# The first attention of a two-block transformer kernel, worked in pairs of heads

## The chip, the core and the metric

The kernel runs on one NeuronCore of one Trainium2 chip. The metric is the device time of one execution in microseconds (us). The engines are named as in the profile: PE is the TensorE matmul, PEld its weight load, DVE is VectorE, ACT is ScalarE, POOL is GpSimd and SP is SyncE, which here only issues DMAs. PEclk is the TensorE clock that the throttle granted, 1.00 for 2.4 GHz and 0.50 for 1.2 GHz.

## The reference

Two blocks of a transformer run over 256 tokens of width 1024. The change touches one place, the attention of the first layer (16 query heads of 64 channels, four key and value heads, each shared by four query heads). Cut to what matters, and without the batch axis:

```
q, k, v = split(x @ w_in); rotary embedding on q and k
score = sum over index heads of iw * relu(iq . ik / 8), causal
sel   = top 64 keys of each query by score           # a mask, the same for all 16 heads
for each of 16 heads h, with key head g = h // 4:
    logits = q_h k_g^T / 8, masked by sel and by causality
    p      = softmax(logits)
    o_h    = p v_g
out = concat(o_h) @ w_o
```

After it come layer norms, an MLP, a gated linear attention, a second MLP, and a second block with four branches (two of them attentions), cross attention and a feed-forward. None of these changes.

## The kernel before

Activations lie transposed: channels on the 128 partitions, 256 tokens along the free axis, in blocks of 128 channels (qT has 8 such blocks, so block p holds heads 2p and 2p+1, one in partitions 0 to 63, the other in 64 to 127). Weights stream through a ring of four SBUF buffers in 183 units of 16 tiles; ACT rounds each unit to whi (L906), DVE takes the rest wlo (L1307), and each product is three matmuls (L422 to L424). A product unit writes one of four PSUM banks, lin0 to lin3. JOB numbers every use of these banks in program order; the function bank makes PE wait until the fourth job before has been read out (semaphores evac0 to evac3), and filled makes a reader wait for job_done. Four more banks, att0 to att3, serve the attentions.

Each engine runs its own instruction stream, in the order in which it is written. The part in question:

1. The units of q (ups("q")), whose banks ACT copies to qT (L921), while DVE picks the 64 keys of each query (L1528, L1529) and makes the additive mask selbias.
2. Four rope steps for q, two blocks of qT each. PE multiplies by a permutation (L620), and DVE combines in three operations (L1495, L1496, L1498).
3. The 16 heads, one unit u each, over steps s = 0 to 18 (att_step). PE does the scores of unit s into att0 or att1, the transposes of unit s-2 into att2 and the values of unit s-3 into att3. In the scores only the 64 partitions of that head take part; the first half of the queries sees 128 keys, the second 256. kswap is kT with its two halves of partitions exchanged, for the heads whose keys lie in the other half. DVE (att_neg, L1436) adds the mask to the negated scores and takes their minimum; ACT (att_exp, L973) takes the exponential and, in a further instruction, its row sum; DVE (att_scale, L1445 to L1453) inverts the sums and scales the probabilities; ACT copies the transposes to SBUF (L982) and the result, after the values (L589), to qT (L987). Three of the four rope steps of DVE stand between its first heads.
4. keep_warm(9), nine matmuls on the identity that nobody reads (L497), and the units of the output projection ao. ACT splits qT to xh (L926) and DVE to xl (L1317), a quarter at a time, and the first unit (unit_first) waits for each quarter.

The matmuls on full fp32 operands (scores, values, keep_warm, rope) appear in the trace as two MATMUL records each, transposes as one.

Of the kernel before, what the change touches and what calls it, by code (L numbers as in the profile page):

```python
# [17 lines left out]
P = 128  # L18
S = 256
D = 1024  # L20
# [46 lines left out]
def plan():  # L67
# [24 lines left out]
    for i in range(4):  # L92
        add("rope", 4 + i)
# [88 lines left out]
def build(nc, units_d, x_d, mem_d, pos_d, vec_d, const_d, narrow_a_d, narrow_b_d, narrow_f_d, w_a2_d, b_fgt_d, lam_d, out_d):  # L182
# [4 lines left out]
    with ctx:  # L187
# [39 lines left out]
        def stage(*tensors):  # L227
# [4 lines left out]
         top8) = stage(  # L232
# [3 lines left out]
            ("selbias", [P, 2, S]), ("rbuf0", [P, 512]), ("rbuf1", [P, 512]), ("rtmp", [P, 2, S]), ("top8", [P, 8]))  # L236
# [46 lines left out]
        pT_psum, pT_sb, pv_psum, o_done = sem("pT_psum"), sem("pT_sb"), sem("pv_psum"), sem("o_done")  # L283
        z_summed, centered, squared, normed = sem("z_summed"), sem("centered"), sem("squared"), sem("normed")
# [71 lines left out]
        UNITS_ATT = [("A", i, None) for i in range(16)] + [("D", j, t) for j in range(4) for t in range(2)] \  # L356
            + [("F", i, None) for i in range(8)] + [("X", j, None) for j in range(4)]
        ATT0 = {k: [u[0] for u in UNITS_ATT].index(k) for k in "ADFX"}
# [10 lines left out]
        def att_rows(u):  # L369

            k, i, t = UNITS_ATT[u]
            return slice(64 * (i % 2), 64 * (i % 2) + 64) if k in "AF" else slice(0, P)
# [5 lines left out]
        def att_out(u):  # L378
            k, i, t = UNITS_ATT[u]
            return {"A": qT, "D": aqT, "F": fqT, "X": xqT}[k][att_rows(u), i // 2 if k in "AF" else i, att_cols(u)]  # L380
# [30 lines left out]
        def _(pe):  # L411
# [132 lines left out]
            def att_logits(u):  # L544
                k, i, t = UNITS_ATT[u]
                if free_after(u, "AFX"):
                    pe.wait_ge(neg_ready, free_after(u, "AFX"))
                for m in range(2):
                    o = att_scores(u, m)
                    w = att_keys(u, m)  # L550
                    q = slice((m if t is None else t) * P, (m if t is None else t) * P + P)
                    r = att_rows(u)
                    if k == "A":
                        pe.wait_ge(roped, 5 + i // 4)
                        keys = kT if i // 4 % 2 == i % 2 else kswap
                        last = mm(o, qT[r, i // 2, q], keys[r, i // 8, 0:w], start=True, stop=True)  # L556
                    elif k == "D":
# [18 lines left out]
            def att_values(u):  # L576
                k, i, t = UNITS_ATT[u]
                pe.wait_ge(pT_sb, u + 1)
                if free_after(u, "AF"):
                    pe.wait_ge(o_done, free_after(u, "AF"))  # L580
                for n, (m, b) in enumerate(att_blocks(u)):
                    o = att[3][att_rows(u), m * P:(m + 1) * P]
                    if k == "A":
                        v = v_tok[:, b, 64 * (i // 4):64 * (i // 4) + 64]
                    elif k == "F":
# [13 lines left out]


# [37 lines left out]
            for i in range(4):  # L638
                rope(4 + i, [JOB["q", i]], qT[:, 2 * i:2 * i + 2, :])
            pe.wait_ge(kswapped, 2)  # L640
            evacuated(pe, JOB["v", 0])
            for s in range(16 + 3):
                att_step(s, ATT0["A"], 16)
# [247 lines left out]
        def _(act):  # L891
# [134 lines left out]
            for s in range(16 + 3):  # L1026
                att_step(s, ATT0["A"], 16)
            split("ao", qT, lambda c: act.wait_ge(o_done, 4 * c + 4))
# [148 lines left out]
            act.wait_ge(o_done, 24)  # L1177
# [20 lines left out]
            for i in range(4):  # L1198
# [3 lines left out]
                if i == 0:  # L1202
                    branch_split(2, fqT, lambda c: act.wait_ge(o_done, 32))
# [80 lines left out]
        def _(dve):  # L1284
# [137 lines left out]
            def att_neg(u):  # L1422
# [5 lines left out]
                for m in range(2):  # L1428
                    w = att_keys(u, m)
                    if k == "A":  # L1430
                        mask = selbias[:, m, 0:w]
                    elif k == "X":
# [101 lines left out]
            for s in range(16 + 1):  # L1534
                att_step(s, ATT0["A"], 16)
                if s < 3:
                    rope(5 + s, two(qT, 1 + s))
                if s == 3:
                    next_low("q", 3)
            for c in range(4):  # L1540
# [499 lines left out]
```

## Time and profile before

| | us |
|---|---|
| median of 3 runs | 1396.02 |
| lowest, highest | 1394.32, 1397.08 |
| the profiled execution | 1394.16 |
| its span in the trace | 1392.3 |

| engine | busy, share of the span |
|---|---|
| PE | 95% |
| PEld | 91% |
| DVE | 67% |
| ACT | 45% |

In the 40 slices of the page PE is nearly full everywhere, and its clock is 0.9 or 1.0 in all but two slices: the third and fourth (about 70 to 140 us) show 7 and 5. The first attention lies there, from 83.2 to 144.5 us.

### The profile page before, as it was taken

The page shows a single profiled execution, that of the slowest core. Times are in us where ns is not written, and L with a number is a line of the kernel's source. Part 1 is how long each engine was busy: PE and PEld are TensorE (multiplying, and loading weights), DVE is VectorE, ACT ScalarE, POOL GpSimd, SP SyncE. Part 2 cuts the span into 40 slices and gives each one's busy share as a digit, 9 for nine tenths or more (in the row PEclk, how much of TensorE's full clock was granted, in tenths as well). Part 3 has the DMA queues.
Part 4 walks back from the last instruction along what each step waited for, and adds up shares of the span by engine and source line. Part 5 has one row for each costly group of instructions (what it writes and reads, how often), then busy time and mean ns, then how long its engine had stood idle before and what let it go on. Part 6 is the DMA issues. An engine that isn't in the chain of part 4 may idle for free.

```text
span 1392.3 us, 25125 instructions
## 1 busy us (share of the span) xinstructions
PE 1326.4 (95%) x10604; PEld 1272.3 (91%) x10604; DVE 928.1 (67%) x1448; ACT 627.4 (45%) x805; POOL 0.2 (0%) x4
## 2 busy tenths in 40 slices
PE   6889999999998899999999999999899999999897
PEld 6866999999998799999999999889898989999797
DVE  6783576466647767646665458888876665999943
ACT  5334454354444244534435444454445455555431
POOL 0000000000000000000000000000000000000000
PEclk9975999999999899999999999999999999999999
DMA  8320325545334133554532543334445241444430
GB/s 330 115 91 0 122 104 198 184 178 191 115 122 152 61 121 105 198 184 179 195 138 94 209 159 120 118 127 150 141 172 203 92 152 61 152 181 157 175 121 31
DMA packets 28361, 198.41 MB, mean 142 GB/s; under 512 B 3296, under 2 KB 3808, under 8 KB 4592
## 3 DMA queue, kind: packets, MB, share of 16 engines
q1 hardware_dynamic: 27072, 194.00, 38.7%
q10 hardware_dynamic: 1200, 3.14, 0.6%
q8 instruction: 66, 1.08, 0.3%
q14 instruction: 23, 0.19, 0.0%
HBM read 196.08 MB, written 1.05 MB: 142 GB/s over the span
## 4 chain that ended last, share of the span: by engine, by line
PE 69%; DVE 23%; ACT 3%; issue 3%; DMA 1%; DVEq 0%; ACTq 0%
PE lin L422 19%; PE lin L424 18%; PE lin L423 18%; DVE wlo L1307 7%; DVE conv L1748 3%; PE lin L504 2%; PE att L589 2%; PE att L497 2%; DVE fconv L1922 1%; PE att L556 1%; ACT whi L906 1%; PE att L573 1%; DVE fconv L1921 1%; DVE fconv L1923 1%; PE lin L527 1%
## 5 line engine op out<-in xcount | busy, mean ns | idle before, releaser
L422 PE MATMUL lin<-xh,whi 128*128 128x256 f32 x1936 | 556.2, 287 | 17.2 <-DVE xl L1317 11.8
L1307 DVE TENSOR_TENSOR wlo<-raw,whi 128x2048 fp32r<-128x2048 f32 x183 | 418.7, 2291 | 215.2 <-ACT whi L906 214.0
L423 PE MATMUL lin<-xl,whi 128*128 128x256 f32 x1936 | 550.8, 284 | 0.0
L424 PE MATMUL lin<-xh,wlo 128*128 128x256 f32 x1936 | 550.5, 284 | 0.0
L906 ACT ACTIVATE whi<-raw 128x2048 fp32r<-128x2048 f32 x183 | 348.5, 1906 | 179.5 <-PE lin L424 172.7
L422 PEld LDWEIGHTS lin<-xh,whi 128*128 128x128 f32 x1936 | 375.0, 194 | 21.4 <-DVE wlo L1307 10.6
L423 PEld LDWEIGHTS lin<-xl,whi 128*128 128x128 f32 x1936 | 375.0, 194 | 0.1
L424 PEld LDWEIGHTS lin<-xh,wlo 128*128 128x128 f32 x1936 | 374.5, 193 | 0.0
L422 PE MATMUL lin<-fh,whi 128*128 128x256 f32 x512 | 143.4, 280 | 0.0
L423 PE MATMUL lin<-fl,whi 128*128 128x256 f32 x512 | 142.8, 279 | 0.0
L424 PE MATMUL lin<-fh,wlo 128*128 128x256 f32 x512 | 142.8, 279 | 0.0
L424 PEld LDWEIGHTS lin<-fh,wlo 128*128 128x128 f32 x512 | 96.3, 188 | 0.0
L422 PEld LDWEIGHTS lin<-fh,whi 128*128 128x128 f32 x512 | 96.1, 188 | 0.0
L423 PEld LDWEIGHTS lin<-fl,whi 128*128 128x128 f32 x512 | 95.8, 187 | 0.0
L1748 DVE SCALAR_TENSOR_TENSOR conv<-upad,vec,conv 128x256 f32<-128x256 f32 x120 | 58.1, 484 | 3.9
L497 PE MATMUL att<-consts 128*128 128x128 f32 x464 | 57.0, 275 | 0.0
L422 PE MATMUL lin<-gh,whi 128*128 128x256 f32 x176 | 50.7, 288 | 6.4 <-DVE gl L1937 6.4
L497 PEld LDWEIGHTS att<-consts 128*128 128x128 f32 x464 | 54.6, 192 | 0.4 <-issue 0.2
L973 ACT ACTIVATE pr<-lg,nmax 128x128 f32<-128x128 f32 (+1 forms) x72 | 32.4, 452 | 48.5 <-DVE nmax L1436 43.5
L422 PE MATMUL lin<-whi,xh 128*128 128x256 f32 x176 | 50.7, 288 | 0.0
L423 PE MATMUL lin<-wlo,xh 128*128 128x256 f32 x176 | 50.5, 287 | 0.0
L424 PE MATMUL lin<-whi,xl 128*128 128x256 f32 x176 | 50.5, 287 | 0.0
(309 smaller groups left out, 1645.5 us busy)
## 6 DMA issues: line engine op xcount, KB each, us to landing
raw<-units_dram SPq DMA_DIRECT2D x183, 1024.0 KB, 4.8
h<-x_dram SPq DMA_DIRECT2D x1, 1024.0 KB, 6.8
memT<-mem_dram ACTq DMA_DIRECT2D x1, 1024.0 KB, 4.8
out_dram<-h SPq DMA_DIRECT2D x4, 256.0 KB, 2.0
consts<-consts_dram ACTq DMA_DIRECT2D x1, 867.5 KB, 12.2
narrow_a<-narrow_a_dram ACTq DMA_DIRECT2D x1, 544.0 KB, 14.1
vec<-vectors_dram ACTq DMA_DIRECT2D x1, 245.5 KB, 16.9
posi<-pos_dram ACTq DMA_DIRECT2D x1, 128.0 KB, 8.0
```

The source lines that it names most:

```text
L422: mm(out, w[0], a[0], start=first, stop=False)
L423: mm(out, w[0], a[1], start=False, stop=False)
L424: return mm(out, w[1], a[0], start=False, stop=last)
L497: mm(att[0][:, 0:P], ident, ident, start=True, stop=True)
L504: ins = mm(flat[:, (col + t) * width:(col + t + 1) * width], block[:, t * P:(t + 1) * P], ones[:, 0:width], start=first and t == 0, stop=l ...
L527: last = mm(o[:, n, t * P:(t + 1) * P], inv[:, col:col + 1].broadcast_to([P, P]), ident, start=True, stop=True)
L556: last = mm(o, qT[r, i // 2, q], keys[r, i // 8, 0:w], start=True, stop=True)
L589: last = mm(o, v, pT[u % 2][:, n, :], start=b == 0, stop=b == att_keys(u, m) // P - 1)
L906: f(whi[u % RING][:], raw[u % RING][:], ACT.Copy).then_inc(hi_ready, 1)
L973: last = f(pr[u % 2][:, m, 0:w], lg[u % 2][:, m, 0:w], ACT.Exp, scale=-1.0, bias=nmax[:, u % 2, m:m + 1], accum_out=rsum[:, u % 2, m:m + 1])
L1307: v.tensor_tensor(wlo[u % RING][:], raw[u % RING][:], whi[u % RING][:].bitcast(f32), ALU.subtract).then_inc(lo_ready, 1)
L1748: ins = v.scalar_tensor_tensor(out=conv[:, b, :], in0=x, scalar=w, in1=conv[:, b, :], op0=ALU.mult, op1=ALU.add)
```

## The change

The first attention leaves att_step and gets functions of its own that treat two heads, a pair p, in one step. The second block keeps the old code; there only the numbering of its units shifts.

- Scores of a pair (pair_scores) go to two banks of the lin ring, one for each head, and thus become two jobs. The four matmuls alternate between the heads, that is, between partitions 0 to 63 and 64 to 127.
- DVE (pair_neg) does what att_neg did, reads lin, and writes lg0, lg1 for an even pair and pr0, pr1 for an odd one.
- ACT (pair_exp) takes the exponential in place, without row sums. DVE no longer scales the probabilities.
- Transposes go to att0 for the even head and att1 for the odd one, after keep_warm(3) in each pair; ACT copies each to one of four buffers pT0 to pT3.
- The values (pair_values) go to att2 or att3. Beside v times the probabilities they form ones times the probabilities, the row sums, spread over 64 partitions. Each step is eight matmuls instead of the three of each head, of 256 or 128 columns, alternating between output partitions 0 to 63 and 64 to 127.
- DVE (pair_result) takes the reciprocal of the sums out of PSUM (128x256) and multiplies the result by it into qT; ACT's copy of the result goes.
- Two of the four rope products of PE move into steps 2 and 4. Where they stood there is keep_warm(14).

```diff
-    for i in range(4):
-        add("rope", 4 + i)
+    add("rope", 4); add("rope", 5)
+    for p in range(8):
+        if p in (2, 4):
+            add("rope", 5 + p // 2)
+        add("scores", p, banks=2)
...
+            ("pT2", [P, 4, P]), ("pT3", [P, 4, P]), ("amax", [P, 4, 2]), ("asum", [P, S]))
+        scores, apT = lg + pr, pT + [pT2, pT3]
...
+            def pair_scores(p):
+                pe.wait_ge(roped, 5 + p // 2)
+                j = JOB["scores", p]
+                o = [bank(j + e) for e in range(2)]
+                for m in range(2):
+                    w, q = P * (m + 1), slice(m * P, m * P + P)
+                    for e in range(2):
+                        r = slice(64 * e, 64 * e + 64)
+                        keys = kT if p // 2 % 2 == e else kswap
+                        last = mm(o[e][:, m, 0:w], qT[r, p, q], keys[r, p // 4, 0:w], start=True, stop=True)
+                        if m:
+                            last.then_inc(job_done, 1)
+            def pair_transposes(p):
+                for e in range(2):
+                    if p:
+                        pe.wait_ge(a_pT_sb, 2 * (p - 1) + e + 1)
+                    if e == 0:
+                        keep_warm(3)
+                    pe.wait_ge(a_exp, 2 * p + e + 1)
+                    for n, (m, b) in enumerate(((0, 0), (1, 0), (1, 1))):
+                        last = nc.tensor.transpose(att[e][:, n * P:(n + 1) * P], scores[2 * (p % 2) + e][:, m, b * P:(b + 1) * P], ident)
+                    last.then_inc(a_pT_psum, 1)
+            def pair_values(p):
+                pe.wait_ge(a_pT_sb, 2 * p + 2)
+                if p >= 2:
+                    pe.wait_ge(a_done, p - 1)
+                o = att[2 + p % 2]
+                for b in range(2):
+                    q0, n = b * P, 2 - b
+                    for at, w in ((0, v_tok[:, b, 64 * (p // 2):64 * (p // 2) + 64]), (S, ones[:, 0:64])):
+                        for e in range(2):
+                            t = apT[2 * (p % 2) + e][:, 2 * b:2 * b + n, :]
+                            last = mm(o[64 * e:64 * e + 64, at + q0:at + S], w, t, start=b == at == 0, stop=b == 1 and at == S)
+                last.then_inc(a_pv_psum, 1)
...
             ups("q")
-            for i in range(4):
+            for i in range(2):
                 rope(4 + i, [JOB["q", i]], qT[:, 2 * i:2 * i + 2, :])
             pe.wait_ge(kswapped, 2)
             evacuated(pe, JOB["v", 0])
-            for s in range(16 + 3):
-                att_step(s, ATT0["A"], 16)
+            keep_warm(14)
+            for s in range(8 + 2):
+                if s in (2, 4):
+                    i = 1 + s // 2
+                    rope(4 + i, [JOB["q", i]], qT[:, 2 * i:2 * i + 2, :])
+                if s < 8:
+                    pair_scores(s)
+                if 2 <= s:
+                    pair_values(s - 2)
+                if 1 <= s < 9:
+                    pair_transposes(s - 1)
+            pe.wait_ge(a_pT_sb, 16)
             keep_warm(9)
...
-            for s in range(16 + 3):
-                att_step(s, ATT0["A"], 16)
-            split("ao", qT, lambda c: act.wait_ge(o_done, 4 * c + 4))
+            def pair_exp(p):
+                j = JOB["scores", p]
+                for e in range(2):
+                    evacuated(act, j + e)
+                    sc = scores[2 * (p % 2) + e]
+                    for m in range(2):
+                        w = P * (m + 1)
+                        last = f(sc[:, m, 0:w], sc[:, m, 0:w], ACT.Exp, scale=-1.0, bias=amax[:, 2 * (p % 2) + e, m:m + 1])
+                    last.then_inc(a_exp, 1)
+            def pair_transposed(p):
+                for e in range(2):
+                    act.wait_ge(a_pT_psum, 2 * p + e + 1)
+                    if p >= 2 and e == 0:
+                        act.wait_ge(a_pv_psum, p - 1)
+                    f(apT[2 * (p % 2) + e][:, 0:3, :], att[e][:, 0:3 * P].rearrange("p (n q) -> p n q", q=P), ACT.Copy).then_inc(a_pT_sb, 1)
+            for s in range(8 + 1):
+                if s < 8:
+                    pair_exp(s)
+                if s:
+                    pair_transposed(s - 1)
+            split("ao", qT, lambda c: act.wait_ge(a_done, 2 * c + 2))
...
             rope(4, two(qT, 0))
-            for s in range(16 + 1):
-                att_step(s, ATT0["A"], 16)
-                if s < 3:
-                    rope(5 + s, two(qT, 1 + s))
+            def pair_neg(p):
+                j = JOB["scores", p]
+                for e in range(2):
+                    filled(dve, j + e)
+                    if p >= 2:
+                        dve.wait_ge(a_pT_psum, 2 * (p - 2) + e + 1)
+                    for m in range(2):
+                        w = P * (m + 1)
+                        last = v.tensor_tensor_reduce(out=scores[2 * (p % 2) + e][:, m, 0:w], in0=lin[(j + e) % RING][:, m, 0:w], in1=selbias[:, m, 0:w],
+                                                      scale=-64 ** -0.5, scalar=3.0e38, op0=ALU.add, op1=ALU.min, accum_out=amax[:, 2 * (p % 2) + e, m:m + 1])
+                    read_out(last, j + e)
+            def pair_result(p):
+                dve.wait_ge(a_pv_psum, p + 1)
+                if p:
+                    dve.wait_ge(a_done, p)
+                o = att[2 + p % 2]
+                link(v.reciprocal(asum[:], o[:, S:2 * S]))
+                v.tensor_tensor(qT[:, p, :], o[:, 0:S], asum[:], ALU.mult).then_inc(a_done, 1)
+            for s in range(8 + 2):
+                if s < 8:
+                    pair_neg(s)
+                if s in (0, 2, 4):
+                    rope(5 + s // 2, two(qT, 1 + s // 2))
                 if s == 3:
                     next_low("q", 3)
+                if s >= 2:
+                    pair_result(s - 2)
             for c in range(4):
                 low("ao", qT, c)
             residual("ao", "ln0")
```

In the order of instructions, without the counts of semaphores, one round of PE before is three matmul groups for one head. Here are two rounds (heads 3 and 4 scored, att the attention banks, pT the transposed probabilities):

```order
L556 MATMUL att1<-kswap,qT 128x128 [waits roped,neg_ready]
L556 MATMUL att1<-kswap,qT 128x256 [waits roped]
L573 MATMUL att2<-consts,pr1 128x128 [waits pT_sb,p_ready]
L573 MATMUL att2<-consts,pr1 128x128 x2
L589 MATMUL att3<-pT0,v_tok 64x128 [waits pT_sb]
L589 MATMUL att3<-pT0,v_tok 64x128 x2
L556 MATMUL att0<-kswap,qT 128x128 [waits roped,neg_ready]
L556 MATMUL att0<-kswap,qT 128x256 [waits roped]
```

In the changed kernel, the round in which pair 2 is scored and pair 0 gets its values, on PE as well:

```order
L612 MATMUL lin3<-kswap,qT 128x128 [waits evac0,evac3,roped]
L612 MATMUL lin0<-kT,qT 128x128
L612 MATMUL lin3<-kswap,qT 128x256
L612 MATMUL lin0<-kT,qT 128x256
L639 MATMUL att2<-pT0,v_tok 64x256 [waits a_pT_sb]
L639 MATMUL att2<-pT1,v_tok 64x256
L639 MATMUL att2<-pT0,consts 64x256
L639 MATMUL att2<-pT1,consts 64x256
L639 MATMUL att2<-pT0,v_tok 64x128
L639 MATMUL att2<-pT1,v_tok 64x128
L639 MATMUL att2<-pT0,consts 64x128
L639 MATMUL att2<-pT1,consts 64x128
```

The two heads' matmuls now stand next to each other, and the scores wait for ring banks (evac) instead of neg_ready. On DVE, the start of the attention before: rope for block pair 1 stands behind the mask operation of head 0.

```order
L1436 ISA lg0,nmax<-att0,selbias 128x128 [waits lg_ready,roped]
L1436 ISA nmax 128x1
L1436 ISA lg0,nmax<-att0,selbias 128x256
L1436 ISA nmax 128x1
L1495 TENSOR_TENSOR rtmp<-lin1,sinT 128x512 [waits job_done]
```

And DVE in the changed kernel around steps 2 and 3, with the second rope of the stage, the first result and the mask operations of pair 3:

```order
L1564 TENSOR_TENSOR rtmp<-lin2,sinT 128x512 [waits job_done]
L1565 TENSOR_TENSOR qT<-qT,cosT 128x512
L1567 TENSOR_TENSOR qT<-qT,rtmp 128x512 [waits evac2,dve_step]
L1621 RECIPROCAL asum<-att2 128x256 [waits a_pv_psum,roped]
L1622 TENSOR_TENSOR qT<-att2,asum 128x256 [waits dve_step]
L1611 ISA pr0,amax<-lin1,selbias 128x128 [waits a_pT_psum,job_done]
```

The result of pair s-2 stands behind the rope and in front of the mask operations of pair s+1.

## Rows read from the trace of the kernel before

**Rows 1.** The page: span, engines, and the chain that ended last.

```profile
span 1392.3 us, 25125 instructions
PE 69%; DVE 23%; ACT 3%; issue 3%; DMA 1%; DVEq 0%; ACTq 0%
```

**Rows 2.** Windows of the attention: length, busy PE, PEld, DVE, ACT, POOL; PEclk; DMA; GB/s.

```profile
85.00:87.00 2.00, 0.83 (x4) 0.43 (x4) 1.93 (x4) 0.88 (x4) 0.00 (x0) 1.00 0.10 41
87.00:89.00 2.00, 0.82 (x3) 0.50 (x3) 1.96 (x9) 0.98 (x4) 0.00 (x0) 0.65 0.00 0
95.00:120.00 25.00, 25.00 (x85) 16.46 (x85) 10.63 (x50) 11.27 (x40) 0.00 (x0) 0.50 0.12 42
142.00:143.00 1.00, 1.00 (x8) 0.66 (x7) 0.00 (x0) 0.38 (x1) 0.00 (x0) 0.90 0.00 0
```

**Rows 3.** Timeline of PE, the attention: start, duration (us), instruction, idle time before.

```profile
78.36 3.60 PE L620 MATMUL lin<-qT,consts 128*128 128x512 f32 x8
...
83.17 0.34 PE L556 MATMUL att<-kT,qT 64*128 64x128 f32 x1 [1.21 <-DVE qT L1498]
...
83.73 0.38 PE L556 MATMUL att<-kswap,qT 64*128 64x256 f32 x1
84.92 0.92 PE L556 MATMUL att<-kT,qT 64*128 64x128 f32 x4 [0.81 <-DVE nmax L1436]
...
93.75 1.65 PE L556 MATMUL att<-kswap,qT 64*128 64x128 f32 x4
95.33 0.90 PE L573 MATMUL att<-consts,pr 128*128 128x128 f32 x3
96.16 1.54 PE L589 MATMUL att<-pT,v_tok 128*64 128x128 f32 x6
97.63 1.65 PE L556 MATMUL att<-kT,qT 64*128 64x128 f32 x4
...
142.44 0.55 PE L573 MATMUL att<-consts,pr 128*128 128x128 f32 x3
142.92 1.52 PE L589 MATMUL att<-pT,v_tok 128*64 128x128 f32 x12
144.37 2.27 PE L497 MATMUL att<-consts 128*128 128x128 f32 x18
146.40 0.36 PE L422 MATMUL lin<-xh,whi 128*128 128x256 f32 x1
```

**Rows 4.** Timeline of PE, two levels of the gated linear attention, output halves alternating.

```profile
430.50 1.15 PE L694 MATMUL lin<-qk 128*64 128x64 f32 x32 [1.68 <-DVE qk L1615]
...
462.24 1.92 PE L694 MATMUL lin<-gqT,gkT 128*64 128x64 f32 x32
```

**Rows 5.** Timeline of DVE: rope, mask operations, the rest of a weight unit.

```profile
84.78 0.69 DVE L1495 TENSOR_TENSOR rtmp<-lin,sinT 128x512 f32<-128x512 f32 x1
...
86.82 0.29 DVE L1436 CUSTOM_DVE_ANT_0 lg<-att,selbias 128x128 f32<-128x128 f32 x1
...
87.04 0.42 DVE L1436 CUSTOM_DVE_ANT_0 lg<-att,selbias 128x256 f32<-128x256 f32 x1
...
94.57 2.29 DVE L1307 TENSOR_TENSOR wlo<-raw,whi 128x2048 fp32r<-128x2048 f32 x1
```

**Rows 6.** Timeline of ACT: one exponential of each size, and the copy of the transposes.

```profile
97.45 0.40 ACT L973 ACTIVATE pr<-lg,nmax 128x128 f32<-128x128 f32 x1 [0.69 <-DVE nmax L1436]
...
97.85 0.49 ACT L973 ACTIVATE pr<-lg,nmax 128x256 f32<-128x256 f32 x1
...
100.15 0.49 ACT L982 ACTIVATE pT<-att 128x384 f32<-128x384 f32 x1 [1.31 <-PE att L573]
```

**Rows 7.** Groups by shape, DVE: count, busy us, mean ns of the reciprocals there are.

```profile
L1325 DVE RECIPROCAL inv<-dev 128x2 f32<-128x2 f32 x12 | 2.0, 165 | 15.6 <-ACT dev L945 15.6
...
L1325 DVE RECIPROCAL inv<-dev 128x8 f32<-128x8 f32 x2 | 0.4, 198 | 1.3 <-ACT dev L945 1.3
```

**Rows 8.** Windows of the gated linear attention, columns as in rows 2.

```profile
450.00:455.00 5.00, 2.15 (x41) 1.88 (x40) 3.92 (x4) 1.57 (x2) 0.00 (x0) 1.00 0.22 29
455.00:460.00 5.00, 1.83 (x32) 1.64 (x32) 4.93 (x9) 1.06 (x1) 0.00 (x0) 0.62 0.44 185
```

More of the change, by code:

```diff
@@ L231, in build @@
         (narrow_a, qT, kT, kswap, v_tok, iqT, ikT, cosT, sinT, ang, turns, posi, iw, work, selbias, rbuf0, rbuf1, rtmp,
-         top8) = stage(
+         top8, pT2, pT3, amax, asum) = stage(
             ("narrow_a", [P, DB, 136]), ("qT", [P, 8, S]), ("kT", [P, 2, S]), ("kswap", [P, 2, S]),
@@ L235, in build @@
             ("ang", [P, S]), ("turns", [P, S]), ("posi", [P, S], i32), ("iw", [P, 2, 8]), ("work", [P, 2, S]),
-            ("selbias", [P, 2, S]), ("rbuf0", [P, 512]), ("rbuf1", [P, 512]), ("rtmp", [P, 2, S]), ("top8", [P, 8]))
+            ("selbias", [P, 2, S]), ("rbuf0", [P, 512]), ("rbuf1", [P, 512]), ("rtmp", [P, 2, S]), ("top8", [P, 8]),
+            ("pT2", [P, 4, P]), ("pT3", [P, 4, P]), ("amax", [P, 4, 2]), ("asum", [P, S]))
+        scores, apT = lg + pr, pT + [pT2, pT3]
         rbuf = [rbuf0, rbuf1]
@@ L283, in build @@
         pT_psum, pT_sb, pv_psum, o_done = sem("pT_psum"), sem("pT_sb"), sem("pv_psum"), sem("o_done")
+        a_exp, a_pT_psum, a_pT_sb, a_pv_psum, a_done = sem("a_exp"), sem("a_pT_psum"), sem("a_pT_sb"), sem("a_pv_psum"), sem("a_done")
         z_summed, centered, squared, normed = sem("z_summed"), sem("centered"), sem("squared"), sem("normed")
@@ L352, in leave @@
                 self.n, self.g = self.first + times * self.step, None
-        UNITS_ATT = [("A", i, None) for i in range(16)] + [("D", j, t) for j in range(4) for t in range(2)] \
+        UNITS_ATT = [("D", j, t) for j in range(4) for t in range(2)] \
             + [("F", i, None) for i in range(8)] + [("X", j, None) for j in range(4)]
-        ATT0 = {k: [u[0] for u in UNITS_ATT].index(k) for k in "ADFX"}
+        ATT0 = {k: [u[0] for u in UNITS_ATT].index(k) for k in "DFX"}
         def att_keys(u, m):
@@ L371, in att_rows @@
             k, i, t = UNITS_ATT[u]
-            return slice(64 * (i % 2), 64 * (i % 2) + 64) if k in "AF" else slice(0, P)
+            return slice(64 * (i % 2), 64 * (i % 2) + 64) if k == "F" else slice(0, P)
         def att_cols(u):
@@ L379, in att_out @@
             k, i, t = UNITS_ATT[u]
-            return {"A": qT, "D": aqT, "F": fqT, "X": xqT}[k][att_rows(u), i // 2 if k in "AF" else i, att_cols(u)]
+            return {"D": aqT, "F": fqT, "X": xqT}[k][att_rows(u), i // 2 if k == "F" else i, att_cols(u)]
         def att_scores(u, m):
@@ L545, in att_logits @@
                 k, i, t = UNITS_ATT[u]
-                if free_after(u, "AFX"):
-                    pe.wait_ge(neg_ready, free_after(u, "AFX"))
+                if free_after(u, "FX"):
+                    pe.wait_ge(neg_ready, free_after(u, "FX"))
                 for m in range(2):
@@ L552, in att_logits @@
                     r = att_rows(u)
[L553 to L557, printed above, removed]
+                    if k == "D":
                         r = slice(64 * m, 64 * m + 64)
@@ L578, in att_values @@
                 pe.wait_ge(pT_sb, u + 1)
-                if free_after(u, "AF"):
-                    pe.wait_ge(o_done, free_after(u, "AF"))
+                if free_after(u, "F"):
+                    pe.wait_ge(o_done, free_after(u, "F"))
                 for n, (m, b) in enumerate(att_blocks(u)):
                     o = att[3][att_rows(u), m * P:(m + 1) * P]
-                    if k == "A":
-                        v = v_tok[:, b, 64 * (i // 4):64 * (i // 4) + 64]
-                    elif k == "F":
+                    if k == "F":
                         v = fv_tok[:, b, 64 * i:64 * i + 64]
@@ L1176, in _ @@
             gates(0, 0)
-            act.wait_ge(o_done, 24)
+            act.wait_ge(o_done, ATT0["F"])
             for i in range(2):
@@ L1202, in _ @@
                 if i == 0:
-                    branch_split(2, fqT, lambda c: act.wait_ge(o_done, 32))
+                    branch_split(2, fqT, lambda c: act.wait_ge(o_done, ATT0["X"]))
                 elif i == 1:
@@ L1429, in att_neg @@
                     w = att_keys(u, m)
-                    if k == "A":
-                        mask = selbias[:, m, 0:w]
-                    elif k == "X":
+                    if k == "X":
                         mask = const("zero").broadcast_to([P, S])
```

## The prediction, made before the changed kernel ran

> **What bounds the kernel now.** I read the page first. Of the span of 1392.3 us, PE carries 69% of the chain that ended last and DVE 23% [rows 1]. A gain must therefore shorten what PE does, or a place where PE waits. The slices then point to one stretch in which PE is busy and slow. The windows say it plainly: from 95 to 120 us PE is busy all 25 us, at a granted clock of 0.50, while DVE works 10.6 and ACT 11.3 us of them [rows 2]. So the first attention is bound by PE at 1.2 GHz, the lower of its two levels. The timeline of PE gives the period. Scores start at 93.75, transposes at 95.33, values at 96.16, the next scores at 97.63 [rows 3]. That is 1.58 + 0.83 + 1.47 = 3.88 us a head, 7.76 a pair, and this repeats for 12 heads without a gap. The stage runs from 83.17 to the first product of ao at 146.40, 63.2 us. Ahead of the drop of the clock PE had long pauses: 0.83 us of work in 85 to 87 and 0.82 in 87 to 89, in which the clock falls to a mean of 0.65 [rows 2]. It comes back only in 142 to 143 (0.90), when the scores have ended [rows 2].
>
> **What a pair costs after the change, on PE at 2.4 GHz.**
>
> Scores. Once in the trace two heads' scores stand side by side, each in its own half of the partitions. Their eight records start between 83.17 and 83.73 and end at 84.11, 0.94 us for two heads, against 0.92 for one head alone at 84.92 [rows 3]. Two heads in different halves cost as much as one. The end of the last record overlaps the next work, so I take 0.80 of engine time.
>
> Values with sums. They double in number: 2x(256+256+128+128) = 1536 columns for two heads, where the old way has 768. Six old records of 128 columns took 1.47 us at the lower clock, and twelve took 1.52 at the full one [rows 3], 0.127 each. The new 1536 columns are worth 24 such records, 3.04 us in a row. But they alternate between output halves. The trace shows this form in the levels: 32 records of 64 columns in 1.15 us [rows 4], where the same price in a row would be 32 x 0.063 = 2.0. Half is gone, and at the lower clock too (1.92 for 32, rows 4, against 4). I take half of 3.04, 1.5 us.
>
> keep_warm(3): six records at 2.27/18 [rows 3], 0.76. Transposes: three from 142.44 to 142.92 [rows 3], so six are 0.96.
>
> Sum 0.80 + 1.50 + 0.76 + 0.96 = 4.0 us a pair against 7.76. In each round the values wait for ACT's second copy of the transposes (two at 0.38 of pitch, and a semaphore on either side) while only the scores, 0.8, lie between. I add 0.3 for that: 4.3 a round.
>
> **DVE and ACT beside it.** ACT per pair: four exponentials, 0.40 and 0.49 with 0.09 of overlap [rows 6], 1.4 us, and two copies, 0.8. That is 2.2 of 4.3; it loses four sums and two result copies, all hidden. DVE per pair: mask operations, 0.22 us between the starts of the two sizes and some 0.34 for the larger [rows 5], twice, 1.12 us. The scaling of probabilities goes, at no gain, since DVE was idle there. New are a reciprocal of 128x256 and a product from PSUM, which costs like a mask operation, 0.45 with its semaphore.
>
> The reciprocal is the open price. No row has this size. Its floor is an ordinary operation of 128x256, 0.42 [rows 5]. The two small sizes cost 165 ns for 2 columns and 198 for 8 [rows 7], 5.5 ns a column; 256 columns give 0.165 + 254 x 0.0055 = 1.56. The means of few, tiny instructions can hide 40% of a slope, so the upper end is 2.2. I take 1.56, as the only rows of this operation lead there.
>
> By the Trainium skill, page "VectorE: DVE Perf Modes", section "Walkthrough: the 8-slice pipeline in each mode", the reciprocal is an iterated division with a repeat count of 8. Eight cycles for each of 256 columns at the 0.96 GHz that its page "Trainium Kernel Development and Optimization", section "NeuronCore Architecture", gives would be an estimated 2.1 us and set the result near the slow end of my forecast; rows 7 show a dear column (5.5 ns) but not quite that.
>
> With 1.56 a pair costs DVE 1.12 + 1.56 + 0.45 + gaps = 3.2 us, under PE's 4.3. In steps 2 to 4 stand also two ropes at 2.0 each (84.78 to 86.78, rows 5) and one weight rest at 2.2 [rows 5]: 9.6 + 6.2 = 15.8 us against PE's three rounds with two rope products of 0.9 (3.60/4, rows 3), 14.7. DVE falls behind, the next scores wait for banks, and I charge 1.7 us.
>
> **The stage, step by step.** Two rope products of PE end at 80.2 instead of 82.0. keep_warm(14) at 0.253 lasts until 83.7. DVE's first rope ends at 83.02 as before, so the filler costs 0.5. Scores of pair 0 run to 84.5. Scores of pair 1 go to the banks of the two ropes, and the second of these is read by DVE only behind the mask operations of pair 0: 84.5 + 0.45 + 1.12 + 0.62 + a semaphore = 87.0. This wait of 2.5 us is new; the old pauses in the same place sum to 3.2 (0.81 before 84.92, rows 3, and 4 - 0.83 - 0.82 = 2.35 from 85 to 89, rows 2). What is queued behind it on PE are keep_warm and the transposes of pair 0, which need it anyway. Then the first round without values, 2.5, to 89.5; six rounds (s = 2 to 7), 25.8, and two rope products, 1.8, to 117.1; step 8 without scores, 3.2, plus 1.1 of waiting for the copies that no scores hide, to 121.4; step 9, 1.1 + 1.5, to 124.0; DVE's lateness, 1.7, to 125.7.
>
> The hand-over changes too. Before, ao's products start 1.9 us after the last value product (144.5 to 146.4), under keep_warm(9). Now DVE stands between: semaphore 0.4, reciprocal 1.56, product 0.45, the first quarter of xl 0.65, 0.1. ao starts at 128.8 against 146.4. The saving is **17.6 us**. Everything behind ao is the same code and bound as before. The weights of ao's first units are in SBUF long before (the last rest in the stage ends at 96.9, rows 5), so no DMA takes the place.
>
> By reciprocal cost the start of ao is 125.6 (0.42 us; then keep_warm(9) bounds it) or 130.9 (2.2 us; DVE bounds three more rounds): savings 20.8 and 15.5. The profiled execution took 1394.16 us, 1.86 under the median, so the sum is 1376.6 on it and 1378.4 on the median; I give **1378**.
>
> **Rivals.**
>
> 1. *The clock falls in the start-up and comes back.* Pauses like 84.5 to 87.0 stand in the levels: 2.15 us of work in 5 left the clock at 1.00, 1.83 in 5 brought it to 0.62 [rows 8]. Here 84.5 to 89.5 holds 2.5 us. Behind it PE is busy at both clocks, so it should return; some 10 us at half clock cost 5: 1383. For it speaks the place, where it fell before; against it the filler ahead and the denser work.
> 2. *The value products do not share the array.* Then a round is 1.5 longer, 12 us in all, less the 1.7 of DVE, which is then hidden: 1388. Against it are rows 4; for it only that those have 64 columns, not 256.
> 3. *The clock stays at 0.50 through the stage.* This one ends slower. At the lower clock a pair costs scores 1.5 (a head alone has 1.58), values 2.9 (half of 24 x 0.245), filler 1.5, transposes 1.66, 7.6 against 7.76: the second copies and the filler eat all that pairing gives. Added are two rope products inside the stage at twice 0.9 and a slower tail; ao starts near 153: +7, 1403. Before, 50 us of uninterrupted PE work did not lift the clock [rows 2]. Against it: that work always used half the array, scores by rows and values by columns, and the clock came back within three us when only transposes and values were left. It decides slower or faster: with more than about 70% of the stage at 0.50 nothing is gained.
> 4. *The reciprocal is as dear as 2.2 us.* 1380.5 as worked out above.
>
> **How the numbers follow.** Forecast (full clock, shared array, reciprocal between the row's slope and the floor) 0.50; rival 4, 0.22; rival 1, 0.12; rival 2, 0.07; rival 3, 0.08; 0.01 for no change at all. The forecast's own range is 1374 to 1380. The range 1373 to 1388 takes in all but rival 3 and the worst mixtures. Below 0.2% (2.8 us) a measurement of this kernel tells nothing; faster than that come out all but rival 3 and a mixture: 0.89 faster, 0.03 same, 0.08 slower.
>
> **What would show it.** In the profile of the changed kernel the windows from 90 to 125 us should have PEclk 1.00, and rounds of PE 4.3 us apart. Sixteen value records should last about 1.5 us; 3 would be rival 2. The reciprocal of 128x256 has its own row on DVE. PE should pause once for about 2.5 us before the scores of pair 1 (released by DVE's rtmp), and ao start near 129. If PEclk is 0.50 in most of the stage, the forecast is wrong at its root. It would be wrong too if a wait that I hold for hidden, such as ACT's exponentials, comes last in a round.

## The result and the profile after

| | us |
|---|---|
| before, median (4 runs) | 1396.03 |
| changed, median of 4 runs | 1376.47 (1375.75 to 1377.22) |
| changed, profiled execution | 1376.77, span 1375.0 |
| ratio to before | 0.9861, 95% interval 0.9844 to 0.9878 |

The change makes the kernel 19.6 us faster by the medians. The prediction said 1378, within 1373 to 1388.

The windows of the changed kernel, with the columns of [rows 2], show the clock at 1.00, as do all the others from 83 to 130 us; it was 0.50 in 95 to 120 before:

```profile
85.00:87.00 2.00, 0.82 (x8) 0.41 (x8) 1.03 (x7) 0.35 (x2) 0.00 (x0) 1.00 0.79 332
87.00:89.00 2.00, 1.08 (x10) 0.78 (x11) 1.97 (x5) 1.14 (x4) 0.00 (x0) 1.00 0.00 0
91.00:98.00 7.00, 6.98 (x66) 5.01 (x66) 5.79 (x18) 3.41 (x9) 0.00 (x0) 1.00 0.01 2
98.00:105.00 7.00, 5.87 (x51) 4.12 (x52) 6.97 (x19) 3.74 (x11) 0.00 (x0) 1.00 0.42 151
105.00:112.00 7.00, 5.52 (x54) 3.80 (x53) 6.86 (x19) 2.99 (x8) 0.00 (x0) 1.00 0.00 0
```

From 98 to 112 us DVE is busy all but 0.17 us, and PE is no longer full: the bound has moved to DVE there. The timeline of PE answers to [rows 3]: the filler, the first scores, the pause before pair 1, one undisturbed round (pair 3 scored, pair 1 valued), the two pauses in the middle, and the hand-over.

```profile
81.67 3.29 PE L503 MATMUL att<-consts 128*128 128x128 f32 x28
84.89 0.37 PE L612 MATMUL lin<-kT,qT 64*128 64x128 f32 x1
...
87.92 0.34 PE L612 MATMUL lin<-kT,qT 64*128 64x128 f32 x1 [2.10 <-DVE rtmp L1564]
...
95.07 0.37 PE L612 MATMUL lin<-kswap,qT 64*128 64x128 f32 x1
...
95.92 0.65 PE L639 MATMUL att<-pT,v_tok 128*64 128x256 f32 x4
96.40 0.60 PE L639 MATMUL att<-pT,consts 128*64 128x256 f32 x4
...
97.37 0.94 PE L503 MATMUL att<-consts 128*128 128x128 f32 x6
98.14 0.82 PE L624 MATMUL att<-consts,lg 128*128 128x128 f32 x6
98.80 1.02 PE L661 MATMUL lin<-qT,consts 128*128 128x512 f32 x2
...
104.78 0.34 PE L612 MATMUL lin<-kT,qT 64*128 64x128 f32 x1 [1.13 <-DVE rtmp L1564]
...
111.08 0.65 PE L639 MATMUL att<-pT,v_tok 128*64 128x256 f32 x4 [1.38 <-ACT pT L1092]
...
123.71 2.27 PE L503 MATMUL att<-consts 128*128 128x128 f32 x18
...
126.78 0.36 PE L428 MATMUL lin<-xh,whi 128*128 128x256 f32 x1 [0.80 <-DVE xl L1388]
```

The round is 0.85 (scores) + 1.45 (values and sums) + 0.77 (filler) + 0.66 (transposes). The stage lasts from 84.89 to 126.78, 41.9 us, where it was 63.2. On DVE the new operations have these rows:

```profile
L1621 DVE RECIPROCAL asum<-att 128x256 f32<-128x256 f32 x8 | 14.0, 1756 | 3.4 <-PE att L639 3.2
L1622 DVE TENSOR_TENSOR qT<-att,asum 128x256 f32<-128x256 f32 x8 | 3.4, 424 | 0.3
```

The stage is 21.3 us shorter, the profiled span only 17.3. In this execution the stage starts 1.7 us later (84.89 against 83.17). Some 1.35 of it is DVE's first rope step, which ends that much later (84.37 against 83.02), behind a stretch from 30 to 50 us in which the clock was at 0.91 and in the kernel before at 1.00; the rest is the filler ahead of the first scores. Another 2.3 us goes behind the stage, in code that is the same. Windows of the changed kernel, one ahead of the stage and two behind it:

```profile
30.00:50.00 20.00, 20.00 (x141) 17.60 (x142) 11.97 (x17) 6.81 (x9) 0.00 (x0) 0.91 0.41 158
870.00:900.00 30.00, 28.99 (x205) 26.02 (x206) 24.87 (x59) 18.62 (x39) 0.00 (x0) 0.94 0.30 110
980.00:1010.00 30.00, 25.78 (x205) 25.60 (x205) 20.42 (x26) 15.82 (x16) 0.00 (x0) 0.94 0.46 170
```

By the starts of the weight operations (wlo) the changed kernel is 20.2 us ahead up to 890 us, 18.7 at 917 and 17.2 from 1003 on. The first loss follows the short fall of the clock in 870 to 880 (0.83). The kernel before has such falls too (0.83 in 870 to 880 and in 990 to 1000, by its own time), but at other work. In the profile of e8, a kernel of the next section with the same code behind the stage, the clock stays at 1.00 from 870 to 900, and its lead over the kernel before stays at 20.8 us. The fall in 30 to 50 differs from one execution to the next: e1 and e5, with the same code up to there, show 1.00 in it, the other variants 0.91. For the falls behind the stage that stays open. The medians, 19.6 apart, lie between.

### The profile page after: what moved, and what is told of

It reads as the page before. It is cut to its first block, busy times and chain, and to the rows that moved or that the text cites. A ratio compares the mean times of both kernels' runs of the same rounds, so it can differ in the third digit from the quotient of the medians.

```text
span 1375.0 us, 25200 instructions
## 1 busy us (share of the span) xinstructions
PE 1303.0 (95%) x10712; PEld 1259.5 (92%) x10712; DVE 934.1 (68%) x1416; ACT 617.4 (45%) x757; POOL 0.2 (0%) x4
## 4 chain that ended last, share of the span: by engine, by line
PE 70%; DVE 23%; ACT 3%; issue 3%; DMA 1%; DVEq 0%; ACTq 0%
PE lin L428 20%; PE lin L430 19%; PE lin L429 19%; DVE wlo L1378 6%; DVE conv L1841 3%; PE lin L510 2%; PE att L503 2%; DVE fconv L2015 2%; DVE fconv L2014 1%; ACT whi L957 1%; DVE fconv L2016 1%; PE lin L533 1%; DVE fy L2026 1%; DVE fy L2025 1%; PE att L589 1%
## 5 line engine op out<-in xcount | busy, mean ns | idle before, releaser
L503 PE MATMUL att<-consts 128*128 128x128 f32 x540 | 67.8, 277 | 0.0
L503 PEld LDWEIGHTS att<-consts 128*128 128x128 f32 x540 | 63.9, 192 | 2.4 <-issue 2.2
L429 PE MATMUL lin<-gl,whi 128*128 128x256 f32 x176 | 50.1, 285 | 0.0
L430 PE MATMUL lin<-gh,wlo 128*128 128x256 f32 x176 | 50.1, 284 | 0.0
```

The source lines that it names most:

```text
L429: mm(out, w[0], a[1], start=False, stop=False)
L430: return mm(out, w[1], a[0], start=False, stop=last)
L503: mm(att[0][:, 0:P], ident, ident, start=True, stop=True)
```

## The experiments

Each kernel was timed in 4 runs beside the kernel before on the same chip. The chips differ a little: the kernel before had a median of 1396.16 beside e1 to e4, 1396.03 beside e5 to e9 and 1395.61 beside e10 to e13, so the ratios compare better than the medians. All together:

| run | median us | ratio to before, interval |
|---|---|---|
| the changed kernel | 1376.47 | 0.9861 (0.9844 to 0.9878) |
| e1_no_pair_fill | 1374.06 | 0.9848 (0.9827 to 0.9870) |
| e2_no_start_fill | 1376.90 | 0.9865 (0.9848 to 0.9883) |
| e3_no_fill | 1375.85 | 0.9855 (0.9837 to 0.9872) |
| e4_before_fill | 1386.18 | 0.9935 (0.9917 to 0.9953) |
| e10_before_fill_first | 1379.59 | 0.9888 (0.9871 to 0.9905) |
| e5_values_by_head | 1381.36 | 0.9898 (0.9879 to 0.9917) |
| e7_copy_for_reciprocal | 1372.91 | 0.9829 (0.9813 to 0.9846) |
| e8_rope_first | 1374.55 | 0.9848 (0.9832 to 0.9865) |
| e9_scale_before | 1373.78 | 0.9849 (0.9832 to 0.9866) |
| e11_ropes_first_no_fill | 1374.20 | 0.9840 (0.9822 to 0.9858) |
| e12_scale_ropes_first | 1368.29 | 0.9802 (0.9786 to 0.9818) |
| e13_scale_ropes_no_fill | 1369.08 | 0.9811 (0.9795 to 0.9828) |

### What keeps the clock up

**e1_no_pair_fill** leaves out keep_warm(3), **e2_no_start_fill** keep_warm(14), **e3_no_fill** both.

```diff
-                    if e == 0:
-                        keep_warm(3)
...
-            keep_warm(14)
```

> The changed kernel without keep_warm(3) in each pair; keep_warm(14) stays. Theory P (the pairing keeps the clock, because scores and values now use both halves of the array): PEclk stays 1.00 in the stage. A round of PE is 0.77 us shorter, but DVE's mask operations, reciprocal and product (1.12 + 1.79 + 0.34 = 3.3 us a pair) then bound it, so of 8 x 0.77 = 6.2 us only 1 to 3 come back: 1373.5 to 1375.5. Theory F (the fillers keep the clock): PEclk falls to 0.50 in most of the stage and the time rises by some 15 us, to 1385 to 1395.

> The changed kernel without keep_warm(14) ahead of the pairs; keep_warm(3) stays. The scores of pair 0 start about 0.5 to 0.9 us earlier. Theory P: the clock may fall in the start-up, where PE has pauses of over 2 us, but comes back within some 10 us: 1376 to 1381. Theory F: as P, or no fall at all. A third one, that a clock once fallen stays down in the stage as it did in the kernel before: PEclk 0.50 to the end of the stage and 1395 or more.

> The changed kernel without either filler. Theory P: PEclk 1.00 in the rounds at the latest some 10 us after the start, 1373 to 1380. Theory F: 0.50 through the stage; a pair then costs scores 1.5, values 2.9, transposes 1.66 = 6.1 us against 7.76 before, so 1380 to 1388.

The times are those of theory P: taking fillers away never costs more than 0.4 us. But the clock did fall, in e1 and e2 as well. The windows of e3, without any filler:

```profile
86.00:88.00 2.00, 0.29 (x2) 0.33 (x4) 2.00 (x10) 1.49 (x4) 0.00 (x0) 0.79 0.30 127
88.00:90.00 2.00, 2.00 (x12) 1.35 (x11) 1.38 (x5) 0.00 (x0) 0.00 (x0) 0.50 0.00 0
...
94.00:98.00 4.00, 4.00 (x40) 2.79 (x40) 3.78 (x12) 2.24 (x6) 0.00 (x0) 1.00 0.00 0
...
105.00:112.00 7.00, 5.09 (x36) 3.45 (x38) 6.90 (x22) 3.41 (x10) 0.00 (x0) 0.76 0.29 122
```

The clock is at 0.50 in 88 to 90 and at 1.00 from 94 on, so the pairs bring it back by themselves; and a second fall in 105 to 112 passes as well. What the falls cost is about what the fillers cost. That is a draw, not a proof that the pairing is what the clock needs, so the counter-test is on the old layout.

**e4_before_fill** puts fillers into the kernel before, with nothing paired (in e4 in every head of this attention):

```diff
+                if UNITS_ATT[u][0] == "A":
+                    for _ in range(3):
+                        mm(att[2][:, 0:P], ident, ident, start=True, stop=True)
                 for n, (m, b) in enumerate(att_blocks(u)):
...
             evacuated(pe, JOB["v", 0])
+            keep_warm(5)
             for s in range(16 + 3):
```

> The kernel before, with five filler matmuls ahead of its first head and three ahead of the transposes of each head (into the bank of the transposes), nothing paired. Theory F: PEclk near 1.00 in the stage, a head then costs 0.92 + 0.76 + 0.48 + 0.76 = 2.9 us against 3.88, so some 14 us less: 1380 to 1384. Theory P (the half-used array is why the clock stays down): PEclk 0.50 in most of the stage, and a head costs 3.88 + 1.4: some 20 us more, 1410 to 1420.

The windows of e4, columns as in [rows 2]:

```profile
88.00:90.00 2.00, 0.99 (x4) 0.99 (x5) 1.96 (x7) 0.98 (x4) 0.00 (x0) 0.71 0.00 0
92.00:95.00 3.00, 3.00 (x12) 2.04 (x10) 2.90 (x10) 0.69 (x4) 0.00 (x0) 0.50 0.00 0
95.00:100.00 5.00, 5.00 (x31) 3.81 (x31) 3.96 (x11) 3.34 (x12) 0.00 (x0) 0.93 0.24 61
110.00:120.00 10.00, 10.00 (x67) 7.48 (x66) 4.02 (x22) 6.36 (x24) 0.00 (x0) 1.00 0.01 2
```

The mechanism of theory F is right here. The clock falls in 88 to 90, comes back between 95 and 96, and stays at 1.00, and a head takes 2.84 us (scores at 98.95 and at 101.79) though PE does more. Ten us are gained with no head paired. The time, 1386.18, is 2 us above the theory's range, which had no term for the stretch at half clock. **e10_before_fill_first** then takes the fillers away again from head 6 on:

```diff
-                if UNITS_ATT[u][0] == "A":
+                if u < 6:
```

> The kernel before with fillers ahead of the first head (five matmuls) and in the first six heads only (three each). With fillers in all heads the clock rose at about 95 us and a head took 2.84 us. Theory H (the low clock is a state that the start-up sets; once up, the old heads hold it up): from head 6 on a head costs 0.85 + 0.42 + 0.80 = 2.1 to 2.4 us at full clock, and the time is 4 to 7 us under the 1386.2 with all fillers: 1379 to 1382, about as fast as the changed kernel. Theory L (the old heads themselves, with half the array, let the clock fall again whenever no filler runs): PEclk goes back to 0.50 and these ten heads cost 3.88 each: 1394 to 1397.

Theory H holds, at the low end of its range. Windows of e10, columns as in [rows 2], then its timeline of PE, two old heads without filler:

```profile
90.00:92.00 2.00, 2.00 (x10) 1.67 (x10) 1.90 (x8) 0.51 (x2) 0.00 (x0) 0.50 0.00 0
92.00:98.00 6.00, 6.00 (x29) 4.51 (x29) 5.90 (x16) 2.48 (x10) 0.00 (x0) 0.68 0.00 1
98.00:105.00 7.00, 7.00 (x49) 5.32 (x48) 3.56 (x21) 4.26 (x16) 0.00 (x0) 1.00 0.44 150
112.00:120.00 8.00, 8.00 (x50) 5.49 (x51) 4.57 (x28) 6.22 (x23) 0.00 (x0) 1.00 0.00 0
```

```profile
114.02 0.92 PE L556 MATMUL att<-kswap,qT 64*128 64x128 f32 x4
114.87 0.55 PE L576 MATMUL att<-consts,pr 128*128 128x128 f32 x3
115.35 0.87 PE L592 MATMUL att<-pT,v_tok 128*64 128x128 f32 x6
116.15 0.92 PE L556 MATMUL att<-kswap,qT 64*128 64x128 f32 x4
```

The very heads that ran for 50 us at 0.50 in the kernel before hold the clock at 1.00 once it is there, and take 2.13 us each instead of 3.88. It is no chance of one execution: all four runs of e10 have a mean clock of 0.981 to 0.982 over the whole kernel, and the runs of the kernel before beside them 0.964 to 0.968. Five filler matmuls ahead of the stage and three in each of six heads are worth 16 of the 19.6 us; which of the two brings the clock back, no run separates. The remaining 3.1 (1379.59 to 1376.47, intervals just overlapping) is not a clean price of pairing: e10 also runs its first heads at 0.50 until 95 us and pays for its fillers. With both at full clock a round for two heads is 3.7 us against 2 x 2.13 = 4.26, though it holds the sums and a filler.

### Whether the halves share the array

**e5_values_by_head** orders the value products by head:

```diff
-                for b in range(2):
-                    q0, n = b * P, 2 - b
-                    for at, w in ((0, v_tok[:, b, 64 * (p // 2):64 * (p // 2) + 64]), (S, ones[:, 0:64])):
-                        for e in range(2):
+                for e in range(2):
+                    for b in range(2):
+                        q0, n = b * P, 2 - b
+                        for at, w in ((0, v_tok[:, b, 64 * (p // 2):64 * (p // 2) + 64]), (S, ones[:, 0:64])):
```

> The changed kernel with the eight value products of a pair in another order: the four of the even head, then the four of the odd one. Theory S (two products share the array only where the halves alternate in program order): the block of sixteen records grows from 1.46 us to about 2.9, a round by 1.45, 11.6 in eight rounds, of which the 4 to 5 us in which PE waits for DVE or ACT in the stage absorb part: 1383 to 1386. Theory Q (PE's queue reaches across to the other half by itself): at most a tenth of that, 1376 to 1378.

The time lies between the two theories: 4.9 us lost. The timeline of PE in e5 shows one block; it lasts from 107.41 to 109.78, 2.37 us against 1.45.

```profile
107.41 0.65 PE L639 MATMUL att<-pT,v_tok 128*64 128x256 f32 x2
107.89 0.59 PE L639 MATMUL att<-pT,consts 128*64 128x256 f32 x2
108.33 0.44 PE L639 MATMUL att<-pT,v_tok 128*64 128x128 f32 x3
108.55 0.27 PE L639 MATMUL att<-pT,consts 128*64 128x128 f32 x1
108.60 0.38 PE L639 MATMUL att<-pT,v_tok 128*64 128x256 f32 x1
...
109.78 0.94 PE L503 MATMUL att<-consts 128*128 128x128 f32 x6
```

By the start times a 256-column product of the odd head (108.60) begins between two 128-column ones of the even head (108.55, and the first of the three at 108.65). So PE takes the other half's work up early, but only in the middle; alternating in the program is worth 0.9 us a pair.

The windows of e5 show one thing more. Its start-up is the same code as in the changed kernel, both fillers included, and yet its clock fell there and came back:

```profile
86.00:88.00 2.00, 1.44 (x12) 1.13 (x13) 1.93 (x6) 0.79 (x3) 0.00 (x0) 0.97 0.00 0
88.00:90.00 2.00, 2.00 (x11) 2.00 (x10) 0.97 (x8) 1.55 (x5) 0.00 (x0) 0.50 0.00 0
92.00:98.00 6.00, 6.00 (x46) 4.13 (x43) 5.46 (x16) 2.37 (x6) 0.00 (x0) 1.00 0.00 0
```

So keep_warm(14) doesn't keep the clock up for certain: the same start-up code kept 1.00 in the profile of the changed kernel and fell to 0.50 in this one.

### What DVE's new work costs

**e7_copy_for_reciprocal** puts tensor_copy in the place of the reciprocal. It leaves out the division, so its result is not that of the attention.

> The changed kernel with a copy in the place of the reciprocal of 128x256, so the result is multiplied by the sums instead of divided. It measures the reciprocal's excess, 1.76 against about 0.42 us. If DVE's lateness is the cause of PE's pauses ahead of the scores of pair 5 (1.13 us) and of the values of pair 4 (1.38), both go, and the hand-over to ao shortens by 0.8 until keep_warm(9) bounds it: 3.3 us in all, 1372.5 to 1374. If these pauses come from ACT or from banks, only the 0.8 goes: 1375.7.

1372.91, 3.6 us less, as the first case said. In its timeline PE has no pause between 87.75 and 115; both pauses of the middle and the 0.80 in the hand-over were DVE's lateness, although the profile puts one of them down to ACT's copy. ACT itself stood behind DVE there: in the changed kernel it idled 3.04 us until 108.79 for DVE's amax, and made its copies behind these exponentials.

**e8_rope_first** moves DVE's second rope ahead of the mask operations of pair 0, where DVE is idle under keep_warm(14).

```diff
             rope(4, two(qT, 0))
+            rope(5, two(qT, 1))
...
-                if s in (0, 2, 4):
+                if s in (2, 4):
```

> The changed kernel with DVE's second rope step ahead of the mask operations of pair 0 instead of behind them. If PE's pause of 2.1 us ahead of the scores of pair 1 is the wait for the second rope's bank, it goes almost whole; the mask operations of pair 0 start 0.4 us later: 1374.3 to 1375.3. If only the clock of the start-up counts or the pause moves to the transposes of pair 0, no change: 1376 to 1377.

1374.55, as the first case said: the pause of 2.10 us is gone, and 0.67 is left ahead of the first transposes. The intervals of e8 and the changed kernel overlap, so the 1.9 us rest on the timeline as much as on the time.

**e9_scale_before** undoes the second part of the change, the sums by products with ones and the division at the end, and keeps the pairs.

```diff
-                    pe.wait_ge(a_exp, 2 * p + e + 1)
+                    pe.wait_ge(a_scaled, 2 * p + e + 1)
...
-                if 2 <= s:
-                    pair_values(s - 2)
-                if 1 <= s < 9:
-                    pair_transposes(s - 1)
+                if 2 <= s < 10:
+                    pair_transposes(s - 2)
+                if 3 <= s:
+                    pair_values(s - 3)
...
+            def pair_scale(p):
+                dve.wait_ge(a_exp, 2 * p + 2)
+                at = 2 * (p % 2)
+                link(v.reciprocal(arinv[:, at:at + 2, :], asum[:, at:at + 2, :]))
+                for e in range(2):
+                    for m in range(2):
+                        sc = scores[at + e][:, m, 0:P * (m + 1)]
+                        last = v.tensor_scalar(sc, sc, arinv[:, at + e, m:m + 1], None, ALU.mult)
+                    last.then_inc(a_scaled, 1)
```

> One part undone, with the pairs, banks and fillers kept: the row sums come from the exponentials again (four more accumulator reads on ACT), DVE inverts them (one reciprocal of 128x4 a pair) and scales the probabilities ahead of the transposes; the products with ones go; the transposes stand two pairs behind the scores and the values three. PE's round is 0.85 + 0.75 + 0.77 + 0.75 = 3.1 us, DVE's 1.12 + 1.3 + 0.42 = 2.85. If these decide, the rounds shorten by about 1 us each and one more round is added: 1369 to 1372. If the loop of transposes, mask operations and scaling decides instead (each waits for the other), a round stays near 4.3 and the added round makes it slower: 1377 to 1381.

1373.78, between the cases. Its PE waits three times for the bank that a rope step of DVE reads (the first time 2.10 us, ahead of 87.84), and in 105 to 112 us the clock is down to 0.76:

```profile
95.19 0.34 PE L612 MATMUL lin<-kswap,qT 64*128 64x128 f32 x1 [2.90 <-DVE rtmp L1564]
106.34 0.34 PE L612 MATMUL lin<-kT,qT 64*128 64x128 f32 x1 [2.10 <-DVE rtmp L1564]
```

The last three kernels put every rope step of DVE ahead of the mask operations of its round:

```diff
+                if s in (0, 2, 4):
+                    rope(5 + s // 2, two(qT, 1 + s // 2))
                 if s < 8:
                     pair_neg(s)
-                if s in (0, 2, 4):
-                    rope(5 + s // 2, two(qT, 1 + s // 2))
```

**e11_ropes_first_no_fill** does so on the changed kernel without keep_warm(3).

> The changed kernel without keep_warm(3) in the pairs and with all three rope steps of DVE ahead of the mask operations of their round, where they stood behind. Each of the two edits alone gave 1374.06 and 1374.55 (there only the first rope moved) against 1376.47. If the pauses of PE for rope banks (2.1 + 1.1 us) and the fillers are separate costs they add: 1371 to 1373. If DVE's sum (1.12 + 1.79 + 0.34 a pair, three ropes, one weight rest: 34.4 us) bounds the stage either way, no more than one of the two gains stays: 1373.5 to 1375.

1374.20, the second case: the gains of e1 and e8 don't add. That DVE's sum bounds the stage fits this, but no run tests it alone; one pause of PE grew to 3.26 us ahead of the values of pair 3, and the clock fell twice.

**e12_scale_ropes_first** does so on e9.

> The kernel with the probabilities scaled ahead of the transposes (1373.78), with all three rope steps of DVE ahead of the mask operations of their round. PE's pauses there were 2.10, 2.90 and 2.10 us, each for the bank that a rope step reads, and the clock fell in 92 to 112. If these pauses were the cause of both, 4 to 6 us go: 1368 to 1370. If the pauses only move to the mask operations, 1373 to 1375.

1368.29, as the first case said, and 8.2 us under the changed kernel; the intervals of the ratios lie apart, from e9's too: this version beats both. The clock stays at 1.00, and ao starts 2.0 us behind the last values, since DVE has only a copy left there. The timeline of PE:

```profile
100.53 0.34 PE L612 MATMUL lin<-kT,qT 64*128 64x128 f32 x1 [0.57 <-DVE rtmp L1564]
103.67 1.07 PE L624 MATMUL att<-consts,pr 128*128 128x128 f32 x6 [1.35 <-DVE pr L1630]
116.16 1.57 PE L639 MATMUL att<-pT,v_tok 128*64 128x256 f32 x16
117.67 2.27 PE L503 MATMUL att<-consts 128*128 128x128 f32 x18
119.70 0.36 PE L428 MATMUL lin<-xh,whi 128*128 128x256 f32 x1
```

**e13_scale_ropes_no_fill** is e12 without keep_warm(3).

> As the run before, and without keep_warm(3) in the pairs. PE's round is 0.85 + 0.75 + 0.75 = 2.35 us, so DVE's 2.85 (1.12 + 1.3 + 0.42) or the loop through ACT bounds it: another 1 to 3 us less if the clock holds, 1366 to 1368; if PE's pauses bring the clock down, as in the kernel before, 1370 to 1375.

1369.08, a tie with e12, between the ranges of the two cases. The clock is that of the second case: PE pauses longer, and the clock is 0.80 in 98 to 105 and 0.71 in 105 to 112.

## Why the prediction was right

The forecast rested on a clock of 2.4 GHz through the stage and on products that share the array; both hold in the profile. By its steps:

- Scores of a pair: 0.80 forecast, 0.85 measured. Values with sums: 1.50 and 1.45. Filler: 0.76 and 0.77. Transposes: 0.96 and 0.66 to 0.75 (94.32 to 95.07). The price taken from three transposes in a row, 0.16 each, was too high for six.
- The 0.3 us a round for the second copy did not appear: at 95.92 the values follow the scores at once. With the transposes this makes a round 3.73 instead of 4.3. In the last two rounds the copies cost 0.63 each instead of 1.1.
- The pause before pair 1 was 2.10 (forecast 2.5), with the releaser named. The two pauses in the middle were 1.13 + 1.38 = 2.5 where 1.7 was charged; e7 shows that they are DVE's.
- The reciprocal took 1756 ns, between the 1.56 of the row's slope and the 2.2 of the upper end. A column costs (1756 - 165)/254 = 6.3 ns, where two tiny sizes gave 5.5.
- The hand-over, from the end of the last value products (123.8) to ao (126.8), was 3.0 us, forecast 3.1. Here two sizes cancel: the reciprocal took 0.2 more than forecast, and the 0.4 charged for a semaphore ahead of it did not appear (DVE starts it at 123.82).
- The stage came out 3.2 us shorter than summed (41.9 against 45.1 from the first scores), and 3.4 us that no term held cancelled that: the stage started 1.2 us later than forecast (84.89 against 83.7), and 2.2 us of the lead at ao was lost behind the stage. That the profiled execution came so near, 1376.77 against a sum of 1376.6, is luck. On the medians the gain was 19.6 and not 17.6.

By the Trainium skill, page "VectorE: DVE Perf Modes", section "Walkthrough: the 8-slice pipeline in each mode", the reciprocal repeats its step eight times; the 2.1 us estimated from it is nearly 0.4 above the measured 1.76. The measurement decides: dear, but less so.

One argument was wrong, though not its conclusion. Against rival 3, the stage at half clock, the prediction held that the old heads "always used half the array" and so could not lift the clock, while pairs fill it. It took this for the reason of the low clock. The transposes of the old heads use all 128 rows and columns [rows 3], so "always" is wrong, and e10 refutes the half array as a sufficient reason: the same heads hold 1.00 once they have it. What differs in these heads between the kernel before and e10 is only that the clock had come back ahead of them. Rival 1 (a fall in the start-up and a return) did not happen in the profile of the changed kernel, but it did in those of e1, e2, e3, e5 and e11. In e1 to e3 the time saved with the fillers hid its cost (e3 leaves out eight times 0.77 us and 14 matmuls at the start, and gains 0.6). In e5, with the same start-up code, it shows that the changed kernel escaped rival 1 partly by luck.

The share of each part in the 19.6 us, so far as the runs show: some 16 are the clock, which needed no pairing (e10); some 3 are left for pairing with everything that belongs to it, as the difference to e10 and no experiment of their own, and e10's half clock at its start and its fillers are mixed into them. The sums by products with ones and the division at the end gave nothing that the runs show: e9, which undoes them, is 2.7 us faster by the medians, though with overlapping intervals, and e12, which also moves the ropes, is clearly faster.

## What to carry over

A stage in which PE is busy without a gap and the clock is at 0.50 should first be tried with a few filler matmuls right behind its start-up pauses: here this gave most of what a rewrite gave. When a rewrite has made PE fast, look at once for the engine whose operations stand between a bank and its next use: moving DVE's reads of a bank ahead of its longer work, and scaling 128x256 probabilities instead of inverting 128x256 sums, was worth another 8 us. And a reciprocal belongs on the small side of a product, before its values are spread.

## What the hardware showed that was not expected

- The clock has a memory. In the kernel before it fell when PE had 1.65 us of work in the four from 85 to 89, and nearly 50 us of uninterrupted work did not bring it back [rows 2]; with three fillers a head it was back at about 96 us (e4, e10) and the same work then held it. The Trainium skill, page "TensorE: Matmul & The Clock Gate", section "What's actually happening", says that "the default state is throttled, and activity releases the throttle". This trace agrees only in part: PE was busy without a gap in these 50 us, and the throttle stayed. What it is in the old heads that holds the clock but does not raise it stays open.
- A fall of the clock doesn't have to cost: e1, e3 and e13, without fillers, show falls to means of 0.71 to 0.80 in the middle of the stage and still tie with their filled versions (the changed kernel and e12).
- By the start times PE takes products of the other output half ahead of their place in the program (e5), but that recovers only part: 2.37 us against 1.45 when alternated and an estimated 3.0 in a row (24 times 0.127, from [rows 3]).
- A reciprocal from PSUM of 128x256 takes 1.76 us, four times a product of that size (0.42).
